# A hybrid token mixer on one core: the order of six head units, and the place of the low-rank gate product

## The reference, cut to what matters

```python
hq, hf, hi, hog, gq, gk, gv, gog, glr, ga, gb = jnp.split(h @ w_in, split_at, axis=-1)
z = heads(hf, HG_HEADS)                                   # 4 heads, dk = dv = 128
log_f = jnp.log(jnp.maximum(lbh + (1 - lbh) * sigmoid(z), LOG_FLOOR))
k_hg = (1 - lbh) * sigmoid(-z);  q_hg = silu(heads(hq)) * HG_DK ** -0.5
o_hg, s_hg = chunked_gated_linear_attention(q_hg, k_hg, heads(hi), log_f, s_hg)
o_hg = gated_head_norm(o_hg, hg_onorm, heads(hog))
log_g = log_sigmoid(glr @ w_gk2 + b_gk) / 16              # low rank: 16 columns
o_gla, s_gla = chunked_gated_linear_attention(
    heads(gq) * GLA_DK ** -0.5, heads(gk), heads(gv), heads(log_g), s_gla)  # 4 heads, dk = 64
o_gla = gated_head_norm(o_gla, gla_onorm, heads(gog))
merged = sigmoid(ga) * (o_hg @ w_br_a) + sigmoid(gb) * (o_gla @ w_br_b)
```

## Time and profile before

| | us |
|---|---|
| median of 3 runs | 2095.99 |
| lowest and highest | 2094.69, 2099.94 |
| the profiled execution's own time | 2092.12 |
| its span, first to last instruction | 2090.3 |

### The profile page before, as it was taken

How to read it: one execution, slowest core, us unless ns; L and a number is a source line. 1 busy time by engine, 2 the same in 40 slices (tenths; PEclk the granted TensorE clock), 3 DMA queues, 4 the chain that set the end, 5 groups by cost and what they waited for, 6 DMA issues and landing times. The chain is left out here.

```text
span 2090.3 us, 26409 instructions
## 1 busy us (share of the span) xinstructions
PE 1672.0 (80%) x10674; PEld 1452.5 (69%) x10674; DVE 1237.1 (59%) x1483; ACT 954.8 (46%) x1086; POOL 529.5 (25%) x231
## 2 busy tenths in 40 slices
PE   4589899989989989895696895189999999999810
PEld 2479788977878878784695774077777777777710
DVE  2532464265646565654454556278888888888727
ACT  2623325322625243442202121177877877777613
POOL 0132111210221112120220000425454454454213
PEclk8789799978999999997798897599999999999955
DMA  8722001200211111110534321679999999999536
GB/s 329 249 52 72 23 16 62 82 22 22 65 43 45 43 44 54 32 36 30 199 132 152 114 101 62 198 270 341 345 357 350 349 351 342 345 349 356 224 146 236
DMA packets 191617, 347.00 MB, mean 166 GB/s; under 512 B 20978, under 2 KB 76746, under 8 KB 190412
## 3 DMA queue, kind: packets, MB, share of 16 engines
q1 hardware_dynamic: 174108, 308.42, 42.4%
q10 hardware_dynamic: 7536, 19.08, 2.3%
q0 software_dynamic: 9856, 17.86, 2.3%
HBM read 316.66 MB, written 44.38 MB: 173 GB/s over the span
## 5 line engine op out<-in xcount | busy, mean ns | idle before, releaser
L128 PE MATMUL x_psum_proj<-h_hi,x_w_hi 128*128 128x364 f32 (+1 forms) x1056 | 367.0, 348 | 0.0
L129 PE MATMUL x_psum_proj<-h_lo,x_w_hi 128*128 128x364 f32 (+1 forms) x1056 | 354.9, 336 | 0.0
L130 PE MATMUL x_psum_proj<-h_hi,x_w_lo 128*128 128x364 f32 (+1 forms) x1056 | 354.2, 335 | 0.0
L1633 POOL DMA_INDIRECT scratch_y<-e_y,e_tbl x32 | 141.7, 4429 | 347.0 <-ACT e_y L1684 347.0
L493 POOL CAST x_w_hi<-x_w 128x1024 fp32r<-128x1024 f32 x44 | 54.2, 1232 | 642.7 <-PE x_psum_proj L130 641.3
L128 PEld LDWEIGHTS x_psum_proj<-h_hi,x_w_hi 128*128 128x128 f32 x1056 | 206.0, 195 | 7.2 <-issue 1.1
L129 PEld LDWEIGHTS x_psum_proj<-h_lo,x_w_hi 128*128 128x128 f32 x1056 | 205.8, 195 | 2.7 <-issue 0.5
L130 PEld LDWEIGHTS x_psum_proj<-h_hi,x_w_lo 128*128 128x128 f32 x1056 | 204.9, 194 | 0.0
L1711 DVE TENSOR_TENSOR e_g_lo<-ew_w,e_g_hi 128x4096 fp32r<-128x4096 f32 x32 | 141.6, 4425 | 60.2 <-ACT e_g_hi L1659 60.2
L128 PE MATMUL e_psum_g<-e_g_hi,e_x_hi 128*128 128x512 f32 x256 | 105.7, 413 | 57.0 <-DVE e_x_lo L1715 57.0
L1627 POOL DMA_INDIRECT e_xg<-scratch_h,e_src x32 | 141.1, 4408 | 34.4 <-PE e_psum_x L1750 20.8
(11 more groups left out here) (294 smaller groups left out, 3700.8 us busy)
## 6 DMA issues: line engine op xcount, KB each, us to landing
ew_w<-in_w_e_gate SPq DMA_DIRECT2D x32, 2048.0 KB, 11.5
ew_w<-in_w_e_up SPq DMA_DIRECT2D x32, 2048.0 KB, 8.9
ew_w<-in_w_e_down SPq DMA_DIRECT2D x32, 2048.0 KB, 10.9
c_w<-in_w_ada SPq DMA_DIRECT2D x12, 2048.0 KB, 16.0
x_w<-in_w_in SPq DMA_DIRECT2D x44, 512.0 KB
scratch_gate<-x_x ACTq DMA_DIRECT2D x16, 544.0 KB, 2.7
m_gate<-scratch_gate SPq DMA_DIRECT2D x16, 544.0 KB, 4.4
z_y<-scratch_y SPq DMA_DIRECT2D x8, 1024.0 KB, 8.2
```

The lines of the kernel that those rows point to most:

```text
L128: nc.tensor.matmul(out, lhs[0], rhs[0], start=start, stop=False)
L129: nc.tensor.matmul(out, lhs[0], rhs[1], start=False, stop=False)
L130: return nc.tensor.matmul(out, lhs[1], rhs[0], start=False, stop=stop)
L1633: nc.gpsimd.indirect_dma_start(out=y_d, out_offset=bass.IndirectOffsetOnAxis(ap=tbl[:, e:e + 1], axis=0), in_=y[:, e % 2, :], in_offset=No ...
```

## The change

`UNITS` becomes hg 0, gla 0, gla 1, hg 1, hg 2, hg 3. The stage then opens with hg 0's `z`, and the low-rank product comes behind it, on PE, on ACT, in SP's loads (after the first weight) and in POOL's splits (after the first weight's). ACT's `decay(0)` comes after the low-rank copies instead of behind the logit pieces, and `decay_key(0)` is added behind it, since the first unit is now an hg unit. The two gla units' logits both become filling, gla 0's in hg 0's scoring loop.

```diff
-    UNITS = [("gla", 0), ("gla", 1), ("hg", 0), ("hg", 1), ("hg", 2), ("hg", 3)]
+    UNITS = [("hg", 0), ("gla", 0), ("gla", 1), ("hg", 1), ("hg", 2), ("hg", 3)]
...
         def _(sp):
             raise_to_start(sp, s)
-            sp.dma_start(lr_w[:, :, :], w_cols[:, :, LR:LR + RANK]).then_inc(lr_in, 16)
-            sp.dma_start(gk2[:, :], a["w_gk2"][0]).then_inc(lr_in, 16)
-            sp.dma_start(b_gk[:, :], a["b_gk"].rearrange("l (u p) -> p (l u)", p=P), allow_slow_non_contiguous=True).then_inc(lr_in, 16)
...
                 sp.dma_start(w[:, n % 2], w_cols[:, :, col:col + P]).then_inc(w_in[n % 2], 16)
+                if n == 0:
+                    sp.dma_start(lr_w[:, :, :], w_cols[:, :, LR:LR + RANK]).then_inc(lr_in, 16)
+                    sp.dma_start(gk2[:, :], a["w_gk2"][0]).then_inc(lr_in, 16)
+                    sp.dma_start(b_gk[:, :], a["b_gk"].rearrange("l (u p) -> p (l u)", p=P), allow_slow_non_contiguous=True).then_inc(lr_in, 16)
...
         def _(pool):
-            pool.wait_ge(lr_in, landed(3))
-            nc.gpsimd.tensor_copy(lr_hi[:, :, :], lr_w[:, :, :]).then_inc(lr_split, 1)
...
+                if n == 0:
+                    pool.wait_ge(lr_in, landed(3))
+                    nc.gpsimd.tensor_copy(lr_hi[:, :, :], lr_w[:, :, :]).then_inc(lr_split, 1)
...
         def _(pe):
+            for name in first(0):
+                for c in range(NC):
+                    project(0, name, c)
             pe.wait_ge(lr_split, after(2))
...
             pe.wait_ge(lr_kept, after(NC))
-            for name in first(0):
-                for c in range(NC):
-                    project(0, name, c)
...
         def _(act):
+            for name in first(0):
+                for c in range(NC):
+                    keep(0, name, c)
             for c, (c0, n) in enumerate(COLS):
                 act.wait_ge(lr_done, after(c + 1))
...
             act.wait_ge(lr_in, landed(3))
-            for name in first(0):
-                for c in range(NC):
-                    keep(0, name, c)
-                if name == first(0)[0]:
-                    decay(0)
+            decay(0)
+            decay_key(0)
```

More of the change, by code:

```diff
@@ L481, in _ @@
                 sp.dma_start(w[:, n % 2], w_cols[:, :, col:col + P]).then_inc(w_in[n % 2], 16)
+                if n == 0:
+                    sp.dma_start(lr_w[:, :, :], w_cols[:, :, LR:LR + RANK]).then_inc(lr_in, 16)
+                    sp.dma_start(gk2[:, :], a["w_gk2"][0]).then_inc(lr_in, 16)
+                    sp.dma_start(b_gk[:, :], a["b_gk"].rearrange("l (u p) -> p (l u)", p=P), allow_slow_non_contiguous=True).then_inc(lr_in, 16)
         @block.gpsimd
         def _(pool):
-            pool.wait_ge(lr_in, landed(3))
-            nc.gpsimd.tensor_copy(lr_hi[:, :, :], lr_w[:, :, :]).then_inc(lr_split, 1)
-            pool.wait_ge(lr_split, after(1))
-            nc.gpsimd.tensor_tensor(lr_lo[:, :, :], lr_w[:, :, :], lr_hi[:, :, :].bitcast(F32), ALU.subtract).then_inc(lr_split, 1)
             for n in range(len(loads)):
@@ L495, in _ @@
                 nc.gpsimd.tensor_tensor(w_lo[:, n % 2], w[:, n % 2], w_hi[:, n % 2].bitcast(F32), ALU.subtract).then_inc(w_lo_done, 1)
+                if n == 0:
+                    pool.wait_ge(lr_in, landed(3))
+                    nc.gpsimd.tensor_copy(lr_hi[:, :, :], lr_w[:, :, :]).then_inc(lr_split, 1)
+                    pool.wait_ge(lr_split, after(1))
+                    nc.gpsimd.tensor_tensor(lr_lo[:, :, :], lr_w[:, :, :], lr_hi[:, :, :].bitcast(F32), ALU.subtract).then_inc(lr_split, 1)
         @block.tensor
```

## The result

The changed kernel takes 2103.37 us in the median of 20 runs, the kernel before, run beside it, 2093.62 (20 runs): a ratio of **1.0044, 95% interval 1.0035 to 1.0052**, or 9.2 us (the medians themselves differ by 9.75). It is slower, by more than the 0.3% that can be told from no change. The time lies inside the forecast's range, but the forecast's likeliest case was +1.4 us, within 0.3%, and what came is the size of the slower rival.

The account below looks back on a forecast made before the run. Stage x was taken as bound by PE's own stream; -0.7 (opening) + 1.7 (wait on q) + 0.4 (hg 0's loop) = +1.4 us on a median of 2095.99 gave 2097.4 us, range 2090.5 to 2104.5.

Parts of the forecast that it names:

- slower rival: Half clock in hg 0's loop (+4 us), a dip at q piece 1 (+1.5), v0's weight late (+1.5): 2104.4 us; chance 0.16.
- 1, first matmul later: Stage x's start: PE waits for a 512 KB weight's split instead of a 64 KB one's, +3.4 us.
- as they are, shifted: gla 0's loop, gla 1, hg 1 to 3 and all later stages keep their times and only shift.
- Part 4: hg 0's loop with logits as filling: +0.4 us, near 50.6; bounds -2 and, with half clock in steps 1 and 2, +4.4.
- part 2: Opening blocks: z takes 14.4 us, low rank 13.9, the logits leave; with the later start, -0.7 us.
- sum's upper bound: Whole kernel: -0.7 + 3.2 + 1.5 + 4.4 = +8.4 us, thus 2104.4 us.
- Part 3: First unit's middle: decay starts late, so PE waits for ACT's copy of q piece 1, +1.7 us.
- by the same count later pieces are kept in time: First unit's middle: after q piece 1, DVE's chain runs ahead and PE waits for no further copies.
- part 5: Seams between units: one hg-to-hg seam becomes hg-to-gla, nothing, at most 1 us either way; later units unchanged.
- the two zeros: No cost at the seam from hg 0 to gla 0, and none in the later units.
- v0's weight: First unit's middle: POOL's split ends about 24.1 us after q's start, wanted at 25.7: nothing, or up to +1.5 us.

Follow-up runs that it names:

- e1: The changed kernel with the low-rank product, its loads, split and copies back at the stage's head, only unit order changed; ratio 1.0009 to the kernel before.
- e2: The changed kernel with ACT's first decay ahead of the low-rank copies and its key pass behind the first copy; ratio 1.0011 to the kernel before.
- e10: e8 with e2's early decay of the first unit; ratio 0.9984 to the kernel before.
- e8: The changed kernel with a gla unit's three logit pieces all in step 0 of the loop ahead; ratio 1.0011 to the kernel before.
- e3: The changed kernel with k ahead of the logits as filling in the loops of hg 0 and gla 0; ratio 1.0011 to the kernel before.

## Where the prediction was right and where it was off

Part by part, changed against before, profiled executions:

| part | forecast | measured |
|---|---|---|
| 1, first matmul later | +3.4 | +3.3 |
| 2, blocks up to q's first piece | -4.1 | -4.0 (28.26 for 32.29) |
| 3, waits on q's pieces | +1.7 | +2.7 (1.38 and 1.33) |
| 3, the rest of the first unit's middle, less three projections of 12.1 | 0 | +0.8 |
| 4, hg 0's loop, against the mean of three hg loops, 49.9 | +0.7 | +2.4 (52.2) |
| 5, seam hg 0 to gla 0 | 0 | +2.2 (102.0, for an hg seam of 63.5 and three projections of 12.1) |
| 5, the later units, "as they are, shifted" | 0 | +2.2 in all: gla 0's loop -0.5, seam to gla 1 +1.3, gla 1's loop +1.4 |
| sum | +1.7 | +9.6 |

(Part 4 stands here against the mean of three hg loops; the prediction set its 50.6 against hg 1's 50.2, so its own sum was +1.4. Its terms for part 2 add to -4.0 and not -4.1.)

The time came inside the range, and part of that is luck. The sum's upper bound was +8.4 us and the measured difference 9.2 (7.3 to 10.9). The time itself stays under 2104.4 only because the base was three runs with a median of 2095.99; twenty runs put the kernel before at 2093.62, from which the same bound would be 2102.0.

**Right** were parts 1 and 2 to 0.1 us (no stretch of half clock lay between 118 and 141 us, as said), and with them the reading that the opening's gain of 4 is eaten by a later start. Part 3's first wait came where and as large as said:

```profile
153.43 0.43 PE L128 MATMUL x_psum_proj<-h_hi,x_w_hi 128*128 128x364 f32 x1 [1.38 <-ACT x_q L638]
159.02 0.43 PE L128 MATMUL x_psum_proj<-h_hi,x_w_hi 128*128 128x364 f32 x1 [1.33 <-ACT x_q L638]
```

**Wrong in part 3** was "by the same count later pieces are kept in time". The second wait comes from the meeting of POOL's split with DVE's differences. I took the row of before as if POOL alone would be held. This time POOL was not held, and DVE was:

```profile
152.18 1.22 POOL L490 CAST x_w_hi<-x_w 128x1024 fp32r<-128x1024 f32 x1 [22.57 <-PE x_psum_proj L130]
153.48 2.77 POOL L492 TENSOR_TENSOR x_w_lo<-x_w,x_w_hi 128x1024 fp32r<-128x1024 f32 x1
```

```profile
152.42 1.55 DVE L893 TENSOR_TENSOR x_lev<-x_b 128x544 f32<-128x544 f32 x1
153.90 2.93 DVE L892 TENSOR_TENSOR x_lev<-x_b 128x544 f32<-128x544 f32 x1
156.75 0.71 DVE L893 TENSOR_TENSOR x_lev<-x_b 128x544 f32<-128x544 f32 x1
```

Two differences took 1.55 and 2.93 us instead of 0.72, so level 3 and with it the copy of q's third piece were 3 us later. A rule of the Trainium skill (SBUF — State Buffer, section Who interferes with whom) says that the order of issue decides who of the two blocks, for a whole instruction. The trace agrees on the whole instruction: the 2.93 us difference ended behind the 2.77 us subtraction. On the order it tells less: here the cast started 0.39 us after a difference and was not held, before it started 0.13 us after one and was held through nine.

**Wrong in part 4** was the choice between its bounds: 52.2 us lies between 50.6 and the upper bound. The half clock did last over the loop's first steps, in part, as the slower rival said: 14.9 us of the loop were at half clock, against 10.2 in e1, where the same loop took the forecast's 50.7. No dip came at q's wait: the clock was 1.00 from 139.81 to 191.00.

**Wrong in part 5, and the largest**, were the two zeros. The seam from hg 0 to gla 0 is 2.2 us longer than its parts, 1.7 of it idle: at a gla unit's first output PE waits 6.0 us for the masked scores, for 4.2 in two waits of an hg unit (3.0 and 1.2). Before, one such wait (6.1 us) stood in the opening, so this idle time moved and did not grow. "Stay as they are, shifted" failed for gla 1: its seam and loop took 2.7 us more, with their idle time unchanged (8.8 and 5.6 us).

Behind this stands the step that failed as a whole: the sum was made by adding waits, each at its own length, and the half-clock time of the stage was taken to stay. Idle time did not grow (103.0 for 103.6 us), and half-clock time grew by 13.1. e2 shows what that misses: it takes away 2.7 us of waits and gains 7, with 3.4 of it in gla 1's seam and loop, far behind. e10 against e8 shows it again, with 5.7 us. That the clock over the same instructions differs is shown by the rows of one seam at 0.80, 0.90 and 1.00; what sets it to one or the other stays open.

The slower rival's total, +7 over the forecast, was nearly that of the result, but by the wrong terms: of its three only the half clock in hg 0's loop came, at less than half its price. v0's weight was not late.

## What to carry to other kernels

In a stream that PE bounds, a step that moves can pay twice where it becomes the first: by the load and split that now stand ahead of it, and by the chain (decay, levels) that lost its cover; put that chain beside whatever else PE does there, as e2 did. Where waits of 1 to 7 us and thin matmuls alternate with dense ones, a few us of waits more or less can move the total by more than themselves through the clock: give such a change a range of several us to either side, set it on a base of many runs, and judge it by medians of many runs. Compare idle time and half-clock time of the whole stage first: here they said in two numbers that the loss inside the stage was clock and not waiting.

## What the runs showed of the hardware

- The clock over the first 17 us of the same seam, with the same wait of 2.9 us in it, was 0.80, 0.90 and 1.00 in three kernels, and the seam repeated itself in two executions of one (103.4 and 103.5 us).
- PE busy without a gap for 27.3 us on 64-row scores and 16-row logits ran at a mean clock of 0.57, right behind 25.9 us at 0.89 with 128-row matmuls among them (e3). Busy time by itself did not keep full clock here.
- POOL's cast beside DVE's differences took 7.17 us in the kernel before. In the changed kernel it took 1.22 (1.04 to 1.22 in five others with an hg unit first), and a DVE difference of 0.72 took 2.93. What decides who is held is not shown.
